# Half a unit of expert weights kept on chip, a first gather by quarters, and the last down weights by column halves, in a mixer, cross-attention and MoE step

## What is computed

```python
y = mixer(rmsnorm(x, g_mix), ...);  x = x + y
x = x + cross_attn(rmsnorm(x, g_xattn), mk, mv, w_q, w_xo)
# moe: top 4 of 32 by router logits, softmax over the four
def expert_ffn(xb, w1, b1, w2, b2):
    gu = xb @ w1 + b1                              # 1024 -> 2048
    gate, up = gu[:, :D_EXPERT], gu[:, D_EXPERT:]
    gate = jnp.minimum(gate, SWIGLU_LIMIT)
    up = jnp.clip(up, -SWIGLU_LIMIT, SWIGLU_LIMIT)
    glu = gate * jax.nn.sigmoid(gate * SWIGLU_ALPHA)
    return ((up + 1) * glu) @ w2 + b2              # 1024 -> 1024
```

## Time and profile before

| | us |
|---|---|
| median of 3 runs (lowest, highest) | 1196.09 (1193.36, 1196.84) |
| the profiled execution | 1195.74 |
| its span, first to last instruction | 1193.9 |
| TensorE busy | 1157.0 (97%) |
| VectorE / ScalarE / GpSimd busy | 306.9 / 157.7 / 28.2 |
| DMA, mean over the span | 384 GB/s, 458 MB |

### The profile page before, as it was taken

How to read it: one execution, slowest core, us unless ns; L and a number is a source line. 1 busy time by engine, 2 the same in 40 slices (tenths; PEclk the granted TensorE clock), 3 DMA queues, 4 the chain that set the end, 5 groups by cost and what they waited for, 6 DMA issues and landing times.

```text
span 1193.9 us, 14908 instructions
## 1 busy us (share of the span) xinstructions
PE 1157.0 (97%) x5937; PEld 604.6 (51%) x5937; DVE 306.9 (26%) x638; ACT 157.7 (13%) x242; POOL 28.2 (2%) x63
## 2 busy tenths in 40 slices
PE   9999999999999999999999999999999999999997
PEld 8888888784434344444444343434343434343433
DVE  5124533332121212122222212121212121212124
ACT  2011011031101210121021011101110111010102
POOL 0000000000000000000000000000000000000000
PEclk9999999999999999999999999999999999999999
DMA  9963444998999999999999999999999999999995
GB/s 366 398 238 129 131 155 150 427 390 335 426 426 428 428 428 429 428 428 430 428 429 427 429 429 429 428 428 429 428 429 428 428 430 428 430 427 428 428 428 221
DMA packets 40398, 458.34 MB, mean 384 GB/s; under 512 B 6032, under 2 KB 6800, under 8 KB 8496
## 3 DMA queue, kind: packets, MB, share of 16 engines
q1 hardware_dynamic: 37440, 454.12, 90.7%
q10 hardware_dynamic: 2928, 3.80, 1.0%
HBM read 454.41 MB, written 3.23 MB: 383 GB/s over the span
## 4 chain that ended last, share of the span: by engine, by line
PE 72%; DMA 25%; DVE 1%; ACT 1%; issue 0%; SPq 0%; DVEq 0%; ACTq 0%
PE ps L1307 25%; PE ps L1084 15%; DMA ring<-in_w_dn 14%; PE ps L1425 13%; DMA arena<-in_w_dn 8%; PE ps L1281 7%; PE ps L1298 3%; DMA ring<-in_w_gu 3%; PE ps L1111 2%; PE ps L1318 2%; PE ps L1192 1%; DMA ring<-in_w_k 1%; PE ps L1177 1%; PE ps L1211 1%; PE ps L1167 1%; PE ps L1414 1%
## 5 line engine op out<-in xcount | busy, mean ns | idle before, releaser
L1307 PE MATMUL ps<-ring,arena 128*64 128x512 f32 x1536 | 349.9, 597 | 5.6 <-DMA ring<-in_w_gu 4.8
L1307 PEld LDWEIGHTS ps<-ring,arena 128*64 128x64 f32 x1536 | 103.1, 136 | 200.6 <-issue 184.7
L1084 PE MATMUL ps<-arena,ring 128*128 128x264 f32 (+1 forms) x800 | 178.9, 385 | 0.0
L1425 PE MATMUL ps<-ring,arena 128*64 128x512 f32 x736 | 165.4, 595 | 9.4 <-DMA ring<-in_w_dn 9.4
L1084 PEld LDWEIGHTS ps<-arena,ring 128*128 128x128 f32 x800 | 151.8, 190 | 25.3 <-issue 0.2
L1307 PE MATMUL ps<-arena 128*64 128x512 f32 x512 | 116.9, 598 | 2.8 <-DMA arena<-in_w_gu 2.4
L1020 DVE COPY arena<-ps 64x512 f32<-64x512 f32 x31 | 21.5, 694 | 369.1 <-PE ps L1425 369.1
L1425 PEld LDWEIGHTS ps<-ring,arena 128*64 128x64 f32 x736 | 52.7, 137 | 112.9 <-issue 106.8
L962 DVE TENSOR_TENSOR resid<-resid,ps 128x264 f32<-128x264 f32 x128 | 53.1, 429 | 173.3 <-PE ps L1298 172.8
L1281 PEld LDWEIGHTS ps<-arena 128*128 128x128 f32 x768 | 90.1, 195 | 14.8 <-issue 14.8
L1281 PE MATMUL ps<-arena 128*128 128x128 f32 x768 | 94.5, 280 | 1.8 <-ACT arena L626 1.8
(11 more groups left out here) (201 smaller groups left out, 504.4 us busy)
## 6 DMA issues: line engine op xcount, KB each, us to landing
ring<-in_w_gu SPq DMA_DIRECT2D x92, 2048.0 KB, 32.6
ring<-in_w_dn SPq DMA_DIRECT2D x44, 2048.0 KB, 32.9
arena<-in_w_gu SPq DMA_DIRECT2D x32, 2048.0 KB, 33.7
arena<-in_w_dn SPq DMA_DIRECT2D x14, 2048.0 KB, 32.8
ring<-in_w_in SPq DMA_DIRECT2D x10, 1024.0 KB, 27.5
ring<-in_kc SPq DMA_DIRECT2D x8, 1024.0 KB, 4.8
ring<-in_vc SPq DMA_DIRECT2D x8, 1024.0 KB, 5.1
ring<-in_w_gu SPq DMA_DIRECT2D x8, 1024.0 KB, 8.8
```

The costliest lines, as they stand in the source:

```text
L1084: last = mm(b[:, 0:width], w[:, k, P * (m % 2):P * (m % 2) + P], source(k), start=(k == 0), stop=(k == KT - 1))
L1307: last = mm(ps[64 * h:64 * h + 64, bank + n, :], tile[:, k, SLOTS * half:SLOTS * half + SLOTS], w[:, at:at + 512], start=(k == 0), stop=(k ...
L1425: last = mm(ps[64 * h:64 * h + 64, 4, :], hid[i % 2][:, k, :], w[:, at:at + 512], start=(k == 0), stop=(k == KT - 1))
```

## The change

1. The first 1 MB chunks of `w_k` are sent so that the first half of chunk 1 goes ahead of the second half of the memory rows, and TensorE does the first halves of keys 2 and 3 before the second halves of keys 0 and 1 (`keys`).
2. The odd rows of the last gate-up unit of expert 31 (1 MB, `stash`) are loaded ahead of `kc` chunk 0, into SBUF that nothing else uses, and the unit itself is later loaded by half. SyncE's last steps are split for that.
3. VectorE copies the first two attention probability tiles before it waits for the samples' softmax (`probs_copied`).
4. The sort into even and odd features moves from ScalarE's copies into the addresses to which TensorE's transposes write. The third token tile lies in another place and keeps its 8 real rows alone, so that a memset falls away (and with it one step of `late_zero`).
5. Ahead of the first gate-up stands one gather quarter; the other three come between the halves of the first three units, the gate transposes within the fourth.
6. In odd experts TensorE's order is gather, turn, combine after units 0, 1, 2 and 3 in place of turn and gather after unit 0 and combine after 1 and 2, and ScalarE copies the gathered half before the sigmoid.
7. At the end, the turn of expert 31 lies within expert 30's down rows. Expert 31's down rows go by 256 columns into two banks, 5 and 4; the last quarter of the weights comes by column halves, and each bank has its own copies. The first combine lies between the last two parts.

The diff, cut:

```diff
 FIRST_BANK = 6
-LAST_PARTS = [(0, 2), (2, 4), (4, 6), (6, 7), (7, 8)]
-LAST_BANK = 5
-FINAL_BANKS = (0, 1, 2, 3, 4, 6, 7, 5)
+LAST_PARTS = [(0, 2, 0, 1024), (2, 4, 0, 1024), (4, 6, 0, 1024), (6, 8, 0, 512), (6, 8, 512, 1024)]
+ARENA = 23280
+LAST_BANKS = (5, 4)
+FINAL_BANKS = (0, 1, 2, 3, 6, 7, 5, 4)
...
                 sp.dma_start(mem_raw[:, k:k_end, :], mem_t[:, k:k_end, :]).then_inc(mem_in[part], 16)
                 sp.dma_start(ring[:, 0, 256 * k:256 * k_end], w_k[0, :, 256 * k:256 * k_end]).then_inc(
-                    landed[0] if part == 2 else part_landed[part], 16)
+                    part_landed[part], 16)
+            half = 256 * KT // 2
+            sp.dma_start(ring[:, 1, 0:half], w_k[1, :, 0:half]).then_inc(part_landed[2], 16)
+            sp.dma_start(mem_raw[:, KT // 2:, :], mem_t[:, KT // 2:, :]).then_inc(mem_in[2], 16)
+            for n in range(2):
+                sp.dma_start(ring[:, n, half:], w_k[n, :, half:]).then_inc(landed[n], 16)
...
             for n, (kind, c) in enumerate(FRONT_CHUNKS):
                 if n == 2:
                     sp.dma_start(resid[:], x_t).then_inc(x_in, 16)
-                if n == 0:
+                if n < 2:
                     continue
+                if (kind, c) == ("kc", 0):
+                    rows = w_gu[NE - 1, KT - 2:KT].rearrange("k p n -> (k p) n")
+                    sp.dma_start(stash[:], rows.rearrange("(p j) n -> p (j n)", j=ROWS_GU)[:, SLOT:2 * SLOT]).then_inc(stash_in, 16)
...
-            for part, (k, k_end) in enumerate(LAST_PARTS):
+                        step(again * NE + NE - 4 + i, i, NE - 4 + i, NE - 3 + i, range(UNITS if i < 2 else 3))
+            last_step = turns * 4 + 2
+            unit_free(last_step, 3)
+            n = (STEP_AT[2] + 3) % RING_UNITS
+            rows = w_gu[NE - 1, KT - 2:KT].rearrange("k p n -> (k p) n")
+            sp.dma_start(unit_buffer(n)[:, 0:SLOT],
+                         rows.rearrange("(p j) n -> p (j n)", j=ROWS_GU)[:, 0:SLOT]).then_inc(unit_landed[n], 16)
+            step(last_step, 2, NE - 2, NE - 1, range(4, UNITS))
...
                 elif k == 4:
                     sp.wait_ge(d_done, turns * 4 + 2)
                 u = k // 4
-                columns_of = slice(D * (k % 4), D * (k % 4) + D * (k_end - k))
-                sp.dma_start(unit_buffer((STEP_AT[3] + u) % RING_UNITS)[:, columns_of],
-                             down_rows(NE - 1, u)[:, columns_of]).then_inc(last_landed[part], 16)
+                by_row = [v.rearrange("p (k n) -> p k n", n=D)[:, k % 4:k % 4 + k_end - k, c:c_end]
+                          for v in (unit_buffer((STEP_AT[3] + u) % RING_UNITS), down_rows(NE - 1, u))]
+                sp.dma_start(by_row[0], by_row[1]).then_inc(last_landed[part], 16)
...
-                by_row = h_tok[n // 2][0:rows, 512 * (n % 2):512 * (n % 2) + 512].rearrange(
-                    "t (b j p) -> t b p j", b=2, j=ROWS_GU)
-                nc.scalar.activation(by_row, bank(("htok", n))[0:rows].rearrange("t (b p j) -> t b p j", b=2, j=ROWS_GU),
+                act.wait_ge(grp, G[("htok", n if n < 4 else 5)] + 1)
+                nc.scalar.activation(h_tok[n // 2][0:rows, 512 * (n % 2):512 * (n % 2) + 512], bank(("htok", n))[0:rows],
                                      ACT.Copy, scale=rstd_tok[0:rows, n // 2:n // 2 + 1]).then_inc(tok_copied, 1)
...
             link(nc.vector.tensor_reduce(att_m[:, 8:9], filled("sS", NMEM), AX.X, ALU.max))
             TS(att_m[:, 8:9], att_m[:, 8:9], -1.0 / 16.0, None, ALU.mult).then_inc(max_ready, 1)
+            dve.wait_ge(kv_stored, 32)
+            def copy_probs(h):
+                copy(probs_t[:, h, :, :], filled(("pT", h)).rearrange("p (m q) -> p m q", m=2)).then_inc(probs_copied, 1)
+            for h in range(2):
+                copy_probs(h)
             dve.wait_ge(s_exp, 5)
             link(nc.vector.reciprocal(att_s[:, 8:9], att_s[:, 8:9]))
-            TS(s_s[:], s_s[:], att_s[:, 8:9], None, ALU.mult).then_inc(emptied, 1)
...
+                for k in range(k_first, k_end):
+                    pe.wait_ge(mem_ready, k + 1)
+                    last = mm(bank(("k", m))[:, 0:NMEM], first_keys[:, m // 2, k, P * (m % 2):P * (m % 2) + P],
+                              mem[:, k, :], start=(k == 0), stop=(k == KT - 1))
+                return last
             for part, (k_first, k_end) in enumerate(FIRST_PARTS):
-                pe.wait_ge(landed[0] if part == 2 else part_landed[part], 16)
+                pe.wait_ge(part_landed[part], 16)
                 for m in range(2):
-                    for k in range(k_first, k_end):
-                        pe.wait_ge(mem_ready, k + 1)
-                        last = mm(bank(("k", m))[:, 0:NMEM], first_keys[:, k, P * m:P * m + P], mem[:, k, :],
-                                  start=(k == 0), stop=(k == KT - 1))
-                    if part == 2:
-                        last.then_inc(grp, 1)
-            for m in range(2, KT):
-                project("w_k", m, lambda k: mem[:, k, :], "k")
+                    keys(m, k_first, k_end)
+            pe.wait_ge(part_landed[2], 16)
+            for m in range(2, 4):
+                keys(m, 0, KT // 2)
+            for m in range(4):
+                if m % 2 == 0:
+                    pe.wait_ge(landed[m // 2], 16)
+                keys(m, KT // 2, KT).then_inc(grp, 1)
                 if m == 2:
                     pe.wait_ge(const_ready, CONSTS)
                     sum_squares("mem_ssq", 1, NMEM, 2)
...
                 pe.wait_ge(h_ready, 2 * KT + (8 if n % 2 else 4))
                 for f in range(4):
-                    last = turn(b[0:width, P * f:P * f + P],
+                    pair = b[0:width, 2 * P * (f // 2):2 * P * (f // 2) + 2 * P]
+                    by_row = pair.rearrange("t (j h i) -> t h i j", j=ROWS_GU, h=2)[:, f % 2]
+                    last = turn(by_row,
...
                         if begun and part == 0:
                             pe.wait_ge(p_built if t == 2 else first_p, 1 if t == 2 else t + 1)
-                        last = mm(b[:, P * at:P * at + P], h_tok[t][:, first:first + P], p_hot[:, t, :],
+                        rows = P if t < 2 else NS
+                        last = mm(b[:, P * at:P * at + P], h_tok[t][0:rows, first:first + P], p_hot[0:rows, t, :],
                                   start=(t == 0), stop=(t == TT - 1))
                 return last
-            pe.wait_ge(late_zero, 3)
...
             pe.wait_ge(tok_copied, 6)
-            gather(begin(("ga", 0)), 0, range(2), begun=True).then_inc(ga_filled, 1)
-            gather(begin(("ga", 1)), 0, range(2, 4)).then_inc(ga_filled, 1)
+            def gather_quarter(n):
+                return gather(begin(("ga", n)), n // 2, range(2 * (n % 2), 2 * (n % 2) + 2), begun=(n == 0))
+            gather_quarter(0).then_inc(ga_filled, 1)
             pe.wait_ge(iters_ready, 2)
             end = pe.value_load(iters[0:1, 0:1], min_val=8, max_val=40)
...
-            def gate_up_unit(w, u, tile, half, bank=0):
+            def combine_last(m):
+                if m == 0:
+                    pe.wait_ge(c_added, end * 16 + 1)
+                pe.wait_ge(y_left, end * 4 + (1 if m < 4 else 2))
+                if m >= 2:
+                    pe.wait_ge(y_right, end * 4 + (1 if m < 6 else 2))
+                mm(ps[:, FINAL_BANKS[m], 0:T], y_hot[:, 1, P * m:P * m + P], g_hot[:, 1, :],
+                   start=True, stop=True).then_inc(c_filled, 1)
...
+                    row = w[:, 0:SLOT] if k % 2 == 0 else w[:, SLOT:2 * SLOT] if second is None else second
                     for n in range(2):
                         for h in range(2):
-                            at = SLOT * (k % 2) + D * h + 512 * n
+                            at = D * h + 512 * n
                             last = mm(ps[64 * h:64 * h + 64, bank + n, :], tile[:, k, SLOTS * half:SLOTS * half + SLOTS],
...
             for u in range(4):
-                if u < 3:
-                    pe.wait_ge(ga_copied, u + 1)
-                else:
-                    pe.wait_ge(emptied, NG)
+                pe.wait_ge(ga_copied, u + 1)
                 pe.wait_ge(unit_landed[u], 16)
                 halves = gate_up_unit(unit_buffer(u), u, xg[0], 0, FIRST_BANK)
                 next(halves).then_inc(half_used, 1)
-                if u == 1:
+                if u < 3:
+                    gather_quarter(u + 1).then_inc(ga_filled, 1)
+                else:
                     turn_gates()
-                if u in (1, 2):
-                    gather(begin(("ga", u + 1)), 1, range(2 * u - 2, 2 * u)).then_inc(ga_filled, 1)
                 next(halves).then_inc(w_used if u < 3 else gu_done, 1)
+            pe.wait_ge(emptied, NG)
...
+                                kept = stash
+                            first, last = gate_up_unit(unit(u), u, xg[((i + 1) // 2) % 2], (i + 1) % 2, second=kept)
                             if i == 0:
                                 first.then_inc(half_used, 1)
```

(31 more changed lines are left out.)

121 lines of the change are left out of this document (67 added, 54 removed).

## The result

| | before | after |
|---|---|---|
| median of 4 runs each, us | 1195.73 | 1213.21 (1212.69 to 1213.82) |
| ratio, 95% interval | | 1.0149 (1.0131 to 1.0167) |
| profiled execution, its span, us | 1195.74, 1193.9 | 1212.79, 1211.0 |
| TensorE busy, us | 1157.0 | 1199.3 |

The forecast was 1192.0 (1189.5 to 1196.2). The bulk of the difference, some 20 us, comes from an edit that the prediction passed over in half a sentence. Of the other edits most did what the prediction said or came close to it. The order of the gather quarters did not, by 2 us, and the rest of the change costs TensorE a further 0.36 us for every two experts, which shows in the time only once TensorE is the bound.

The account below looks back on a forecast made before the run. The expert weights' DMA (402.7 MB, 940 us at 428 GB/s) was taken as the bound. Terms of 3.3 + 0.7 + 0.7 + 0 - 0.6 = 4.1 us took 1195.74 to 1191.6, forecast as a median of 1192.0, range 1189.5 to 1196.2.

Parts of the forecast that it names:

- an edit that the prediction passed over in half a sentence: Gather's third token tile: its 8-row stationary tiles, with the dropped memset, were called off the path and worth nothing.
- The order of the gather quarters: One quarter before the first gate-up: starts it at 266.1 instead of 270.2 us; with the token copies, gain 3.3 us.

## What to carry over

An edit inside a line that runs for every expert is priced by its count first, however small it looks: 128 tiles at 0.34 us outweighed every gain. Don't cut the contraction rows of single matmuls among full ones: here the rows of zeros cost nothing, and the cut did. If a short tile must be, put short ones side by side. An edit whose cost hides behind another bound still has that cost, and it shows when the bound moves. Before something is moved off a wait, list all that lies under its cover, register loads included, not only the copy that the wait is named after.

## What the runs showed of the hardware that was not expected

- A matmul of 8 or of 64 contraction rows among ones of 128 costs about 0.34 us for the way there and back (float32, two instructions each, at full clock), and half as many such steps cost 0.77 instead of 1.34 us a half.
- With the same idle time ahead of the gather (1.75 us in the trace), 6 of 11 runs had a lower mean clock (0.995 to 0.997) and 5 did not; their medians are 1195.5 and 1192.5 us.
- TensorE's two register loads let the next matmul start 1.66 to 1.76 us after VectorE had written the value, in all eleven traces in which the loads stood there and the gather had ended by then; with the loads moved away it started 0.90 us after.
- Transposes that write PSUM with 512 bytes between columns run at the pace of contiguous ones, 0.119 us each.
